# One level less for the 32-token group in the recurrence of a two-layer encoder step (float32, one core)

## What is computed

```python
def step(Sm, inp):
    r_t, w_t, k_t, v_t, kk_t, a_t = inp
    sa = jnp.einsum('bhij,bhj->bhi', Sm, kk_t)
    Sm = (Sm * w_t[:, :, None, :] - sa[..., None] * (kk_t * a_t)[:, :, None, :]
          + v_t[..., None] * k_t[:, :, None, :])
    return Sm, jnp.einsum('bhij,bhj->bhi', Sm, r_t)
```

## Time and profile before

| | us |
|---|---|
| median of 3 runs (lowest, highest) | 1995.67 (1992.82, 2000.57) |
| the profiled execution | 1992.57 |
| its span in the profile | 1990.8 |

### The profile page before, as it was taken

The page is one execution under the profiler, slowest core; times in us unless marked ns, Lnnn a source line. Parts: engine busy times, 40 slices in busy tenths (PEclk is TensorE's granted clock), DMA queues, the critical chain, the costliest instruction groups (busy, mean ns, idle before and its releaser), DMA issues.

```text
span 1990.8 us, 37487 instructions
## 1 busy us (share of the span) xinstructions
PE 1891.4 (95%) x16506; PEld 1734.8 (87%) x16506; DVE 988.4 (50%) x1695; ACT 709.9 (36%) x1272; POOL 94.2 (5%) x100
## 2 busy tenths in 40 slices
PE   6998998999999999999999799989998999999997
PEld 5975776899789999999999478759986999999996
DVE  6676455454435544344367745454543455353533
ACT  4443434553334222122344344453533332121222
POOL 2000000200010000000100000002000100000001
PEclk9998999899999999999999799979999999999998
DMA  5110000453012222222222000013610222222221
GB/s 220 66 40 1 4 2 24 163 170 128 32 64 77 94 86 85 96 85 85 85 75 75 8 3 3 3 44 128 222 64 22 75 85 93 89 86 85 96 85 56
DMA packets 38593, 149.51 MB, mean 75 GB/s; under 512 B 4384, under 2 KB 4544, under 8 KB 36768
## 3 DMA queue, kind: packets, MB, share of 16 engines
q1 hardware_dynamic: 36288, 131.05, 19.6%
q0 software_dynamic: 2144, 16.06, 2.1%
HBM read 139.68 MB, written 7.41 MB: 74 GB/s over the span
## 4 chain that ended last, share of the span: by engine, by line
PE 90%; DVE 5%; ACT 3%; issue 1%; POOL 1%; DMA 0%; DVEq 0%; SPq 0%; ACTq 0%; POOLq 0%
PE PS L516 79%; PE PS L636 8%; PE PS L850 1%; ACT hH L975 1%; POOL sq L452 1%; PE PS L944 0%; DVE stat L1662 0%; DVE wL L1353 0%; ACT ell L975 0%; ACT aP L975 0%; ACT sq L975 0%; DVE hL L1362 0%; DVE kf L1529 0%; DVE hT L1787 0%; DMA xT<-x_in 0%
## 5 line engine op out<-in xcount | busy, mean ns | idle before, releaser
L516 PE MATMUL PS<-hH,wH 128*128 128x272 f32 x2272 | 488.4, 297 | 30.4 <-DMA cst<-cst_in 16.2
L516 PE MATMUL PS<-hH,wL 128*128 128x272 f32 x2272 | 476.4, 291 | 0.0
L516 PE MATMUL PS<-hL,wH 128*128 128x272 f32 x2272 | 476.1, 291 | 0.0
L1353 DVE TENSOR_TENSOR wL<-ring,wH 128x1024 fp32r<-128x1024 f32 x238 | 300.9, 1266 | 216.1 <-ACT wH L975 215.8
L516 PEld LDWEIGHTS PS<-hH,wH 128*128 128x128 f32 x2272 | 361.0, 191 | 42.2 <-issue 19.1
L975 ACT ACTIVATE wH<-ring 128x1024 fp32r<-128x1024 f32 x238 | 249.6, 1051 | 334.3 <-PE PS L516 334.3
L516 PEld LDWEIGHTS PS<-hH,wL 128*128 128x128 f32 x2272 | 362.1, 191 | 0.0
L516 PEld LDWEIGHTS PS<-hL,wH 128*128 128x128 f32 x2272 | 360.3, 191 | 0.0
L516 PE MATMUL PS<-hidH,wL 128*128 128x272 f32 x1024 | 212.3, 289 | 0.0
L516 PE MATMUL PS<-hidH,wH 128*128 128x272 f32 x1024 | 211.9, 288 | 0.0
L516 PE MATMUL PS<-hidL,wH 128*128 128x272 f32 x1024 | 211.4, 288 | 0.0
(11 more groups left out here) (279 smaller groups left out, 2478.7 us busy)
## 6 DMA issues: line engine op xcount, KB each, us to landing
ring<-wall SPq DMA_DIRECT2D x238, 512.0 KB, 3.3
lw<-lw_in POOLq DMA_DIRECT2D x2, 2240.0 KB, 9.9
xT<-x_in SPq DMA_DIRECT2D x4, 544.0 KB, 6.5
y_out<-hT SPq DMA_DIRECT2D x8, 272.0 KB, 2.1
mem<-mem_in POOLq DMA_DIRECT2D x2, 1024.0 KB, 5.0
mks<-mks_in POOLq DMA_DIRECT2D x2, 1024.0 KB, 10.3
mvs<-mvs_in POOLq DMA_DIRECT2D x2, 1024.0 KB, 13.5
memk_out<-mkp POOLq DMA_DIRECT2D x2, 1024.0 KB, 5.5
```

The source lines that it names most:

```text
L516: return e.matmul(out, lhsT=a, rhs=b, start=start, stop=stop)
L1353: tt(wL[:, n % SPLIT], ring[:, n % RING], plain(wH[:, n % SPLIT]), ALU.subtract).then_inc(w_lo, 1)
```

## The change

`levels_of(g)` gives the number of levels of a group: `LEVELS` = 6 for the prompt's groups, `DEC.bit_length() - 1` = 5 for the sample's. The list of steps, the semaphore counts and the tests for the last level follow it. Group 4 has no cross 5 and no merge 5; its merge 4 is handled as the last one. The mask table is unchanged.

```diff
+LEVELS = 6
+
+
+def levels_of(g):
+
+    return LEVELS if g < NG - 1 else DEC.bit_length() - 1
...
             lane += [("tokens", g, 0), ("score_l", g, 0), ("score_m", g, 0), ("merge", g, 0)]
-            for b in range(1, LEVELS):
+            for b in range(1, levels_of(g)):
                 lane += [("cross", g, b), ("merge", g, b)]
...
+CROSSES = sum(levels_of(g) - 1 for g in range(NG))
...
-    "cross": (LEVELS - 1) * NG, "cross_out": (LEVELS - 1) * NG, "merge": LEVELS * NG, "merge_out": LEVELS * NG,
+    "cross": CROSSES, "cross_out": CROSSES, "merge": CROSSES + NG, "merge_out": CROSSES + NG,
...
-                            if 0 < b < LEVELS - 1:
+                            if 0 < b < levels_of(g) - 1:
                                 part(bank(2 * x, 64 * w, 64 * w + 64)[r, :], XX[x][r, 1, w, :], P[x][r, w, :], False)
...
-                    if b == LEVELS - 1:
+                    if b == levels_of(g) - 1:
                         for t in range(2):
...
-                    e.wait_ge(s["merge_out"], at(l, "merge_out", nth("merge", g, LEVELS - 1)))
+                    e.wait_ge(s["merge_out"], at(l, "merge_out", nth("merge", g, levels_of(g) - 1)))
...
-                    i = b == LEVELS - 1
+                    i = b == levels_of(g) - 1
```

More of the change, by code:

```diff
@@ L150, in _rec_steps @@
     return slots + lanes[1][-3:], FACTOR_STEPS + alone
-LEVELS = 6
 FACTOR_STEPS = 5
```

## The result

The change is faster: 1982.4 us median of 10 runs (1979.6 to 1991.5) against 1995.7 of the kernel before (10 runs, 1992.8 to 2000.6), ratio 0.9936, 95% interval 0.9924 to 0.9948. That is 13 us less where I had forecast 6, and just under the lower end of the range. A later comparison of the same two kernels gave 0.9943 (0.9924 to 0.9962), with medians of 1985.5 and 1994.2 us. The profiled execution took 1981.6 us, its span 1979.8, 11.0 less than before.

The account below looks back on a forecast made before the run. PE was taken as the bound, busy 1891.4 of 1990.8 us. Layer 0 -2.0, layer 1 -2.4 and clock -1.6 gave -6.0 us, from 1995.7 to 1989.7; range 1983 to 1998.

Parts of the forecast that it names:

- the tail's +3.5: Group norm and remaining attention after the last state product: three more attention steps lengthen it by 3.5 us a layer.
- the paired stretch's +0.6: Two prompt lanes side by side: gains three attention steps, gives up three at its end, net +0.6 us a layer.
- the dip: PE at 0.58 to 0.59 clock where the lanes start: costs 1.6 us a layer; half taken, -1.6 for both layers.
- The products: Group 4's recurrence: 24 fewer PE instructions per layer cut PE's work from 2.74 to 1.07 us, by 1.67.
- The row's price: Merge 4's 16 instructions take 1.07 us, so 0.067 us for each of the removed small products.
- The piece that leaves the first stretch: Cross 5 to group 0's first transpose, products and attention, all leaves: -6.16 us in layer 0, -6.45 in layer 1.
- the light piece: Work in front of group 0's first transposes, holding a 0.64 us wait for DVE; gone after the change.
- the chain from the sums to the Exp: Norm in the tail, on ACT: table load, Ln, table load, Exp take 5.0 us after the second group-norm sum.
- The tail's clock: Same tail work takes 40.2 us in layer 0, 43.8 in layer 1 at half clock; kept unchanged, least trusted.
- the slower rival: Tail falls to half clock early in both layers, dips stay: +2.2 us, 1997.9; chance 0.15.
- Both fast rivals: Dips go and layer 1's tail becomes like layer 0's: 1984.5, chance 0.14; added steps fill tail idle time: 1986.7, 0.10.
- the best of my single cases: Better clock: both dips go, layer 1's tail becomes like layer 0's: -11.2 us, 1984.5; chance 0.14.

Follow-up runs that it names:

- the second profile: The kernel before, unchanged, profiled a second time; that execution took 2002.2 us.
- the first experiment: Changed kernel with two empty steps in place of cross 5 and merge 5, attention placed as in the kernel before; ratio 0.9957 to the kernel before.
- dip experiments: Kernel before, all products kept, one attention step moved from behind merge 5 to in front of cross 5; ratio 0.9979, median 1993.4 us.

## Why the prediction was wrong, step by step

Three terms of the sum failed: the tail's +3.5 was too large, the paired stretch's +0.6 was not there, and the dip was counted half. Together they left the forecast at -6.0 us, less than half of the 13 measured.

**The products: right.** 1.67 us a layer forecast, 1.63 and 1.71 measured apart, 48 instructions fewer. The row's price held, and not the smaller one of 0.6 us estimated from the Trainium skill's page TensorEngine Tiling (Array Packing), section Instruction Overhead. Its 60 cycles, 0.025 us by the estimate, are less than the 0.067 us that these instructions took from start to start.

**The piece that leaves the first stretch: right.** -6.16 and -6.45 forecast, -6.67 and -6.45 measured. The 0.5 us more in layer 0 lie mostly in front of the new merge 4, which starts 0.4 us sooner (193.52 against 193.95) in a part with the same work.

**The paired stretch: the term +0.6 was mis-sized.** With the order of before and no dip (first and dip experiments) it takes 117.51 to 117.56 us, with the order of the change 117.44: -0.1. I had priced the incoming steps from the light piece, where a wait and gaps lie between them, and the outgoing ones from dense rows; that this is where the error comes from is not shown apart.

**The dip: the price near, its chance wrong.** The price was 1.6 us a layer; the traces give 119.16 - 117.56 = 1.6 and 118.79 - 117.52 = 1.3, and 4.0 and 1.4 in the second profile. I took half of it. The rows spoke for the whole: the dip stood at the same place in both layers, behind the same piece, and the change removes that piece. That the light piece alone lets the clock fall is not so, as the first experiment shows; why it falls stays open.

**The tail: +3.5 was mis-sized.** At the same mean clock of 0.87 it went from 40.47 to 42.49, +2.0. Of the 1.5 us between, 1.3 stand in front of the point where PE goes on behind the norm's Exp: 326.26 - 312.95 = 13.3 us after the last state product, where I had 14.6. The step that failed is the chain from the sums to the Exp: it has one load in it, not two, and took 3.3 us instead of 5.0, while the sums came 0.5 us later than I had walked. Behind that point the sum is right by luck, with 5.6 us of work where I had 4.0, and 1.7 us of idle time less where I had 0.5 more.

**The tail's clock: kept as it was, and it moved.** Four tails of the kernel before took 40.47, 44.04, 42.66 and 42.65 us, six of the change 42.49 once and 44.37 to 44.42 five times. The mean difference is +1.6 a layer. In the pair of profiles that I compared, layer 1's tail rose in mean clock from 0.73 to 0.81 and so grew by 0.4 only. That the longer tail falls to the half clock (the slower rival) didn't happen.

**The sum and the range.** Mean of all profiled layers, the three stretches take 205.8 us before and 198.3 after, 15 us for both layers; the medians say 13, and 9 in the later comparison. Of the 9 us by which these 15 pass the forecast, 3.7 are the tail (+3.3 for both layers instead of +7.0), 3.9 the paired stretch with its dip (-4.3 instead of -0.4) and 1.4 the first stretch, where one profile of the kernel before has a half clock of its own. Both fast rivals were right in part and at the same time: the dips went and the added steps filled waits. I had set them side by side as cases that exclude each other, each with its own total. They are independent terms; -4.4 with whole dips (-3.2), no +0.6 (-1.2) and a tail 1.5 shorter in each layer (-3.0) is -11.8, or 1983.9 us. That is below the best of my single cases, 1984.5, from which I had set the range's end at 1983; the measured median, 1982.4, lies 1.5 us further down. A range built from the sum of the fast terms would have ended lower. And I took the level from the median, 1995.7, but the dips from an execution of 1992.6 us, in which they were short. Three later groups of runs of the kernel before have medians of 1996.9 (22 runs), 1997.2 (11) and 1994.2 (23).

## What to carry to other kernels

When a written order gets shorter, what stands beside it moves too: here the removed products are worth 3.3 us and the shift of the attention, with the clock, more than twice that. Price such a shift at both ends and against its neighbours, by trying two or three positions, since the cost of the later end was next to none for three steps and 4 to 10 us a layer for the next three, and a position between the two had the slowest clock. A clock dip that stands behind the same piece in every layer, and in a second profile too, belongs to the kernel's order; if the change removes part of that piece, count the whole dip. And terms that are independent add up in the range.

## What the runs showed of the hardware

A table load of ACT started as soon as ACT was free, while PE was still at the sums that the Ln behind it reads (320.61, with the products from 320.29 to 322.39), and the first Ln followed 1.29 us after the load's start. In the twelve profiles of other kernels, 24 layers, no dip stood at the start of the lanes; in the kernel before it stood in four layers of four, for about 4 us or for 10, behind 4 us in which PE was busy for 3.36, as it was in another kernel without a dip. A half clock of about 3 us also came up within the sample's stretch in 3 of the 28 layers, in three different kernels. The clock of the same tail, in the same order, differed between layers and executions (mean 0.73, 0.76, 0.87), worth 3.6 us between its ends (44.04 and 40.47).
